# A depthwise convolution moved from VectorE to TensorE, in a two-layer hybrid decoder trunk

## What is computed

```python
p = rmsnorm(x) @ odd_w_in              # 1024 -> 1696 + 1024 columns
o_c = rwkv7(p[..., :1696])             # r, k, v (512 each), decay, a, gate (low rank)
o_d = conformer_conv(p[..., 1696:])    # a and gate, 512 channels each
x = x + concat(o_c, o_d) @ odd_w_out

def conformer_conv(h):
    a, gate = split(h)                 # 512, 512
    z = pad(a * sigmoid(gate), 30 zeros in front)
    y[n, ch] = sum_j conv_w[j, ch] * z[n + j, ch] + conv_b[ch]     # 31 taps, each channel by itself
    return silu(layernorm(y))

# rwkv7, per head of 64: S_t = S_{t-1} (diag(w_t) - kk_t^T (kk_t a_t)) + v_t^T k_t,  y_t = S_t r_t
```

## Time and profile before

| | us |
|---|---|
| time of a run, median of 3 | 1414.79 |
| span of the profiled execution | 1408.7 |
| TensorE matmul busy | 1295.4 (92%) |
| VectorE busy | 716.9 (51%) |
| ScalarE busy | 425.5 (30%) |
| GpSimd busy | 519.9 (37%) |
| second mixer, first projection matmul to first output projection tile | 584.9 to 1003.9 |

### The profile page before, as it was taken

How to read it: one execution, slowest core, us unless ns; L and a number is a source line. 1 busy time by engine, 2 the same in 40 slices (tenths; PEclk the granted TensorE clock), 3 DMA queues, 4 the chain that set the end, 5 groups by cost and what they waited for, 6 DMA issues and landing times. The chain is left out here.

```text
span 1408.7 us, 20615 instructions
## 1 busy us (share of the span) xinstructions
PE 1295.4 (92%) x8420; PEld 1034.2 (73%) x8420; DVE 716.9 (51%) x1012; ACT 425.5 (30%) x536; POOL 519.9 (37%) x374
## 2 busy tenths in 40 slices
PE   5899999999999999979798887777899999999997
PEld 4797978888888888856565666564688888888885
DVE  7435365551124534477858888585655511245333
ACT  4547333221222222254234333232432212122110
POOL 4341435554445545431121110110155544455441
PEclk9899999999999999999998999897999999999998
DMA  4321222223222223210010010000022232222321
GB/s 181 113 99 53 80 70 90 90 89 115 94 90 89 89 98 107 94 60 31 31 61 31 2 60 2 31 32 1 30 90 90 89 118 90 90 90 89 107 73 60
DMA packets 16803, 105.65 MB, mean 75 GB/s; under 512 B 1872, under 2 KB 2144, under 8 KB 4832
## 3 DMA queue, kind: packets, MB, share of 16 engines
q1 hardware_dynamic: 16304, 104.03, 21.4%
q10 hardware_dynamic: 432, 0.64, 0.1%
HBM read 102.57 MB, written 2.10 MB: 74 GB/s over the span
## 5 line engine op out<-in xcount | busy, mean ns | idle before, releaser
L484 POOL TENSOR_TENSOR w_lo<-w_raw,w_hi 128x512 fp32r<-128x512 f32 x368 | 511.1, 1420 | 846.3 <-ACT w_hi L497 296.8
L841 PE MATMUL ps<-h_hi,w_hi 128*128 128x512 f32 x696 | 285.1, 410 | 11.8 <-POOL w_lo L473 11.8
L841 PE MATMUL ps<-h_lo,w_hi 128*128 128x512 f32 x696 | 273.9, 394 | 0.0
L841 PE MATMUL ps<-h_hi,w_lo 128*128 128x512 f32 x696 | 273.5, 393 | 0.0
L841 PEld LDWEIGHTS ps<-h_hi,w_hi 128*128 128x128 f32 x696 | 132.6, 190 | 53.0 <-issue 14.1
L572 ACT ACTIVATE w_hi<-w_raw 128x2048 fp32r<-128x2048 f32 x50 | 95.6, 1912 | 201.8 <-PE ps L841 148.5
L841 PEld LDWEIGHTS ps<-h_hi,w_lo 128*128 128x128 f32 x696 | 132.3, 190 | 28.5
L841 PEld LDWEIGHTS ps<-h_lo,w_hi 128*128 128x128 f32 x696 | 132.5, 190 | 28.1 <-issue 2.7
L841 PE MATMUL ps<-f_hi,w_hi 128*128 128x512 f32 x384 | 151.7, 395 | 0.0
L841 PE MATMUL ps<-f_lo,w_hi 128*128 128x512 f32 x384 | 151.7, 395 | 0.0
L841 PE MATMUL ps<-f_hi,w_lo 128*128 128x512 f32 x384 | 151.7, 395 | 0.0
(11 more groups left out here) (300 smaller groups left out, 1991.2 us busy)
## 6 DMA issues: line engine op xcount, KB each, us to landing
w_raw<-in_weights SPq DMA_DIRECT2D x93, 1024.0 KB, 4.9
outT<-x SPq DMA_DIRECT2D x8, 256.0 KB, 2.2
x<-in_xT SPq DMA_DIRECT2D x6, 256.0 KB, 7.4
masks_f<-in_masks SPq DMA_DIRECT2D x1, 768.0 KB, 10.9
x<-in_xT ACTq DMA_DIRECT2D x2, 256.0 KB, 5.6
w_raw<-in_weights SPq DMA_DIRECT2D x1, 512.0 KB, 6.5
low_w<-in_low_w SPq DMA_DIRECT2D x1, 512.0 KB, 11.6
sgu_ln<-in_sgu_ln SPq DMA_DIRECT2D x1, 512.0 KB, 3.6
```

What stands on the lines that cost most here:

```text
L484: piece = pool.tensor_tensor(w_lo[:, j, at], w_raw[:, j, at], w_hi[:, j, at].bitcast(f32), SUB)
L841: mm = pe.matmul(bank(gb(g) if isinstance(i, int) else g % 2), w, r, start=(k == 0 and m == 0), stop=(k == K - 1 and m == 2))
```

## The change

The convolution becomes matmuls. For a channel group of 128, the stationary operand is a 128 x 128 matrix with two diagonals for each half of its rows. For pair j of 16, rows a = 0..63 carry tap 2j to output column a and tap 2j - 1 to column a + 64; rows b = 64..127 carry tap 2j to column b and tap 2j - 1 to column b - 64. The moving operand is z from position 2j on. So the even taps of a channel are summed in one half of a bank's partitions, the odd taps in the other half, one position off. The two halves of the rows are two matmuls into two banks, `gb(g)` and `gb(g + 1)`; each product is again made of three. 16 pairs make 8 steps `("conv", c, q)` of 12 matmuls of 64 rows and 512 columns. The diagonal matrices are built on the host and lie in four further 1 MB chunks among the weights (numbers 22, 24, 26, 28 of `ROWS`, each taking the place of two tiles).

z is written to `z`, copied to `z_hi` by ScalarE (in `low`), and `z_rest` on VectorE makes `z_lo`. After the last step of a group, `conv_out` on ScalarE copies the even halves to `cv` with the bias and the odd halves to `odd`, and issues two DMAs that move `odd` by 64 partitions and one position to `odd_up`; `conv_sum` on VectorE, placed five steps later, adds it to `cv`. The order of the tiles is new, and quarters or conv steps also stand after `dx` (`DX_N`). Steps per iteration: 24, 24, 24, 16; eight conv steps stand in the start. The taps' columns leave `cols`.

```diff
-MIX1 = [2] * 11
+MIX1 = [2] * 15
-ROWS = [0, 2, 4, 3, 14, 15, 5, 7, 6, 1, 16, 17, 8, 10, 9, 18, 19, 11, 13, 12, 20, 21]
+CONV = [22, 24, 26, 28]
+PAIRS = 16
+ROWS = [0, 2, 14, 15, 4, 3, 22, 23, 5, 7, 6, 16, 17, 8, 24, 25, 1, 10, 9, 11, 13, 12, 18, 19, 26, 27, 20, 21, 28, 29]
...
+        def pairs_of(c):
+            return [("conv", c, q) for q in range(8)]
+
+        ORDER1 = [("slice", t, q) for q in range(4) for t in (0, 2)] + [("stat",)] + quarters([14]) + [("spread",)] \
+            + quarters([15])[:2] + [("zw", 0)] \
+            + quarters([15])[2:] + [("za", 0), ("decay_v", 0, 0), ("ksq", 0)] + quarters([4])[:2] \
+            + [("decay", 0, 1), ("decay_v", 0, 1)] + quarters([4])[2:] + [("ks", 0), ("ks_v", 0), ("decay", 0, 2)] \
+            + [("decay_v", 0, 2)] + quarters([3]) + [("dyn", 0, 0)] + pairs_of(0)[:4] \
+            + [("dyn", 0, 1)] + pairs_of(0)[4:6] + [("bonus", 0)] + pairs_of(0)[6:]
+        FILL = {0: quarters([5, 7, 6, 16, 17, 8]), 1: pairs_of(1) + quarters([1, 10, 9, 11]),
+                2: quarters([13, 12, 18, 19]) + pairs_of(2), 3: quarters([20, 21]) + pairs_of(3)}
+
+        TX_N = {0: [1] * 6, 1: [1] * 6, 2: [1] * 5 + [0], 3: [1, 0, 1, 1, 1, 1]}
+        DX_N = {0: [1] * 6, 1: [1] * 6, 2: [1] * 5 + [0], 3: [1, 0, 1, 1, 1, 1]}
+        STATE_N = {0: [1] * 6 + [0, 0], 1: [1] * 6 + [0, 0], 2: [1] * 8, 3: [0] * 8}
...
-                ORDER1 += [("scores", c, i)] + fill(SCORE_N[c][i])
-            ORDER1 += taps[0]
+                ORDER1 += [("scores", c, i)] + fill(1)
             for lv in range(1, LEVELS):
-                ORDER1 += [("tx", c, lv, 0), ("tx", c, lv, 1)] + mid[lv] + fill(LEVEL_N[c][lv - 1])
-                ORDER1 += [("dx", c, lv, 0), ("dx", c, lv, 1)] + end[lv] + taps[lv]
+                ORDER1 += [("tx", c, lv, 0), ("tx", c, lv, 1)] + mid[lv] + fill(TX_N[c][lv - 1])
+                ORDER1 += [("dx", c, lv, 0), ("dx", c, lv, 1)] + end[lv] + fill(DX_N[c][lv - 1])
...
+            def conv_out(c):
+                g = g1(CONV[c])
+                act.wait_ge(s("gemm_done"), g + 2)
+                if c:
+                    act.wait_ge(s("odd_moved"), 32 * c)
+                act.activation(cv[0:64, c, :], bank(gb(g))[0:64], ACT.Identity, bias=col("conv_b", c)[0:64])
+                act.activation(odd[64:128, :], bank(gb(g))[64:128], ACT.Copy).then_inc(s(f"gemm_evac{g % 2}"), 1)
+                act.activation(cv[64:128, c, :], bank(gb(g + 1))[64:128], ACT.Identity, bias=col("conv_b", c)[64:128])
+                act.activation(odd[0:64, :], bank(gb(g + 1))[0:64], ACT.Copy).then_inc(s(f"gemm_evac{(g + 1) % 2}"), 1)
+                act.wait_ge(*evacuated(g))
+                act.wait_ge(*evacuated(g + 1))
+                if c:
+                    act.wait_ge(s("cv_done"), c)
+                act.dma_start(odd_up[0:64, 1:SEQ], odd[64:128, 0:SEQ - 1]).then_inc(s("odd_moved"), 16)
+                act.dma_start(odd_up[64:128, 1:SEQ], odd[0:64, 0:SEQ - 1]).then_inc(s("odd_moved"), 16)
...
+            def conv(c, q):
+                g = g1(CONV[c])
+                n = N_MIX1 + POS1[CONV[c]] // 2
+                if q == 0:
+                    pe.wait_ge(s("lo_done"), n + 1)
+                    pe.wait_ge(s("z_lo_done"), c + 1)
+                    pe.wait_ge(*freed(g))
+                    pe.wait_ge(*freed(g + 1))
+                for j in range(2 * q, 2 * q + 2):
+                    at, t = slice(P * j, P * j + P), slice(2 * j, 2 * j + SEQ)
+                    for m, (w, v) in enumerate(((w_hi, z_hi), (w_lo, z_hi), (w_hi, z_lo))):
+                        done = []
+                        for i, r in enumerate(COLUMN_HALVES):
+                            done += [pe.matmul(bank(gb(g + i)), w[r, n % 2, at], v[r, t], start=(j == 0 and m == 0),
+                                               stop=(j == PAIRS - 1 and m == 2))]
...
+            def z_rest(c):
+                dve.wait_ge(s("z_hi_done"), c + 1)
+                dve.wait_ge(s("zeroed"), 6)
+                if c:
+                    dve.wait_ge(s("gemm_done"), g1(CONV[c - 1]) + 2)
+                at = slice(TAPS - 1, TAPS - 1 + SEQ)
+                tt(z_lo[:, at], z[:, :], F(z_hi[:, at]), SUB).then_inc(s("z_lo_done"), 1)
+
+            def conv_sum(c):
+                g = g1(CONV[c])
+                dve.wait_ge(*evacuated(g))
+                dve.wait_ge(*evacuated(g + 1))
+                dve.wait_ge(s("odd_moved"), 32 * (c + 1))
+                tt(cv[:, c, 1:SEQ], cv[:, c, 1:SEQ], odd_up[:, 1:SEQ], ADD).then_inc(s("cv_done"), 1)
...
-            def taps(c, a, b):
-                for j in range(a, b):
...
-                        stt(cv[:, c, :], zpad[:, j:j + SEQ], col("conv_w", TAPS * c + j), cv[:, c, :], MUL, ADD)\
-                            .then_inc(s("tap_done"), 1)
```

More of the change, by code:

```diff
@@ L197, in build @@
             om_mu = sb("om_mu", [P, 14])
+            z_hi = sb("z_hi", [P, SEQ + TAPS + 1], f32r)
+            z_lo = sb("z_lo", [P, SEQ + TAPS + 1], f32r)
+            odd = sb("odd", [P, SEQ])
+            odd_up = sb("odd_up", [P, SEQ])
         ps = ctx.enter_context(nc.psum_tensor("ps", [P, 8, 512], f32))
@@ L316, in quarters @@
             return [("slice", t, q) for t in tiles for q in range(4)]
[L318 to L327, removed]
@@ L402, in build @@
                 held += [step[1]]
+            if step[0] == "conv" and step[2] == 7:
+                held += [CONV[step[1]]]
             scaled_yet = scaled_yet or step[0] == "spread"
@@ L410, in build @@
             for t in held:
+                if t in CONV:
+                    order += [("conv_out", CONV.index(t))]
+                    continue
                 order += [("evac_a", t), ("evac_q", t)]
@@ L425, in build @@
                 pieces += [("cut", N_MIX1 + POS1[step[1]] // 2 + 2, part) for part in range(4)]
+            if step[0] == "conv" and step[2] == 7:
+                pieces += [("cut", N_MIX1 + POS1[CONV[step[1]]] // 2 + 2, part) for part in range(4)]
         ORDER1 = order + pieces
+        order, later = [], []
+        for step in ORDER1:
+            order += [step] + [other for left, other in later if left == 1]
+            later = [(left - 1, other) for left, other in later if left > 1]
+            if step[0] == "low" and step[1] >= 15 and step[1] % 2 == 1:
+                later += [(1, ("z_rest", (step[1] - 15) // 2))]
+            if step[0] == "conv_out":
+                later += [(5, ("conv_sum", step[1]))]
+        ORDER1 = order
         def mu_col(t):
@@ L1792, in _tok, with _conv @@
     return w[:, c0:c0 + 256].reshape(KD, P, 256).transpose(1, 0, 2).reshape(P, 2048)
+def _conv(w, c):
+    t = np.zeros((P, PAIRS, P), np.float32)
+    a = np.arange(64)
+    b = a + 64
+    for j in range(PAIRS):
+        t[a, j, a], t[b, j, b] = w[2 * j, P * c + a], w[2 * j, P * c + b]
+        if j:
+            t[a, j, b], t[b, j, a] = w[2 * j - 1, P * c + a], w[2 * j - 1, P * c + b]
+    return t.reshape(P, 2048)
 def _down(w, half, d):
```

61 lines of the change are left out of this document (29 added, 32 removed).

## The result

The change makes the kernel slower: 1427.93 us (median of 4 runs, 1424.96 to 1432.01) against 1413.28 (1411.06 to 1415.5); ratio 1.0116, 95% interval 1.0094 to 1.0138, or 16 us. The forecast was 1408. The profiled execution's span is 1426.9 us.

The account below looks back on a forecast made before the run. TensorE's work, and VectorE where taps stand ahead of updates, were taken to bound the kernel by turns. Iterations -13.8, start +4.6 and dearer pairs +2.5 sum to -6.7 us: 1408 us, own range 1398 to 1418, full range 1388 to 1442.

Parts of the forecast that it names:

- Price of a step: TensorE's conv steps: a pair of half-row matmuls takes 0.243 us, a step 1.57 us plus 0.08, like a projection quarter.
- Taps off VectorE, XT waits gone: Iterations 0 to 3: VectorE loses 25 us of taps each, so late X/XT updates (8.7, 7.9, 7.0, 7.2 us) stop idling TensorE.
- What stays idle, 4.5 us an iteration: TensorE in the iterations: 4.5 us stay idle in each of iterations 0 to 2, 9.5 in iteration 3.
- The DMA, "hidden": Moving odd taps by 64 partitions: lands in 2.2 us, VectorE waits for it five steps later, about 6 us: no cost.
- Clock, 70% given back: Iterations 0 to 3: less idling returns 70% of the clock loss, 4.5, 3.7, 6.0 and 3.9 us.
- Before iteration 0, +4.6: The stage's start: 50.7 us less 9.0, plus 11.1 for eight steps and 2.5 of bank wait, gives 55.3.
- Rival 2, idle is refilled: Iterations: updates stay late, ScalarE is late for TX; half of 56 us idle stays: 1418, or 1431 without clock gain; chance 0.24.

Follow-up runs that it names:

- e6: e1 with the end of a tile's evacuation (ScalarE's part, VectorE's last product) and conv_out moved behind a level's TX copies; ratio 1.0005 to the kernel before.
- e9: e1 with the edits of e5 and e6 together; ratio 0.9964 to the kernel before.
- e11: e9 with e10's order, state-step evacuations behind the state update, rounding only behind a TensorE step and not directly ahead of TX, G or U copies; ratio 0.9916.
- e14: e11 with the bonus behind all four steps of tile 5 and conv_out(3) behind the first U copy; ratio 0.9892 to the kernel before, 1397.2 us.
- e4: The kernel before with 29 of each group's 31 taps left out and nothing added to TensorE; ratio 0.9760, 34 us less than before.
- e1: The changed kernel with ScalarE copying the odd taps straight to the other 64 partitions, without the two DMAs; ratio 1.0042 to the kernel before.
- e2: The changed kernel with the DMA kept and conv_sum of groups 0 to 2 placed 16 steps behind conv_out instead of 5; ratio 1.0070 to the kernel before.
- e3: The changed kernel with one pair of taps per conv step instead of two (half of the products left out); ratio 0.9985 to the kernel before.
- e10: e1 with tiles 1 and 5 ahead of iteration 0 in place of conv(0), which follows in iteration 0; ratio 1.0055 to the kernel before.
- e13: e11's queues with the old tile order ahead of iteration 0, four added steps there and four more in iteration 3; ratio 1.0035 to the kernel before.
- e7: e1 with the reciprocal chain (ks_v) behind tile 3's evacuation and the bonus behind the conv steps; ratio 1.0049 to the kernel before.
- after: The changed kernel itself, as profiled, without follow-up edits; 1427.93 us, ratio 1.0116 to the kernel before.
- e5: e1 with no piece of weight rounding between or directly ahead of a level's TX copies on ScalarE; ratio 1.0011 to the kernel before.
- e8: e1 with conv_out(3) placed behind the first U copy of iteration 3; ratio 1.0057 to the kernel before.

## Why the prediction was wrong

- *Price of a step*: right. Pitch 0.230, forecast 0.243; work 284.4 against 282.1 us.
- *Taps off VectorE, XT waits gone*: right (from 30.9 to 0.2 us at the levels, 3.3 to 0.5 at the state steps), VectorE at 41 to 45 us in iterations 0 to 2 as said. Two readings of the prediction are off without effect: VectorE's tenths in slices 18 to 27 are 7785888888, and in iteration 3 the taps were half of VectorE's work, not 30 to 40%.
- *What stays idle, 4.5 us an iteration*: **this step failed.** It stayed 35.0 us in place of 23.0. I reasoned from busy shares ("ScalarE is busy 31 of 92 us ... neither sets an iteration's length") and listed, apart from the four copies of conv_out(3), only waits that the old trace already had. e6, e9, e11 and e14 show what was missing: what stands ahead of the TX and G copies in ScalarE's queue once TensorE no longer pauses. e4 shows that in the old order, even without any new work, 33 us stay.
- *The DMA, "hidden"*: wrong. It cost with its issues some 10 us (e1), a part of them, by e2's median 6, as VectorE's standstill. Five steps of the order are 6 us, but counted from where ScalarE takes up conv_out; copies (2.6 us), issues (0.5 to 1.3 each) and landing (2.4) used them up. I had priced a landing of 2.2 us from the earlier trace rows and not the way to it.
- *Clock, 70% given back*: wrong, 36% (25.8 to 16.6). The loss goes with the idle time, but loosely: 8.3 us with 15.6 idle (e14), about what I had forecast for 23; 9.7 with 28.6 (e1), 14.4 with 34.3 (e3), yet 16.0 with 26.2 (e10) and 7.9 with 29.5 (e13). What else moves it stays open.
- *Before iteration 0, +4.6*: +9.4. The work of the eight steps was right (11.3 us at the upper clock, forecast 11.1). The idle time fell by 1.9 us and not by 4.7, since the bank wait was 5.8 and not 2.5: I had taken the evacuation of the earlier trace rows, without the reciprocal ahead of it. And the clock gave nothing back, where I had 1.8. How far the wait can be mended is open: e7 shortens it and the start, e10 takes it away and meets 7.1 us for rx instead. In e13 the start, with the old order of tiles and four steps more than before, took 53.9 us against 50.7 before and 61.1 in e11: the four steps took the place of the old wait for rx, for 3.2 us.
- *Rival 2, idle is refilled*, is what happened, for one of the reasons that it gave (ScalarE late for TX; the updates on VectorE were not late). It sized the idle at half of 56 us and the clock at half or nothing, 1418 to 1431. That 1427.9 lies within is partly luck: the idle time was 35 us and not 28, and 5 us came in the start, which it had left alone. 0.24 was too little for a case in which each delay was visible in the order list.

## What to carry to other kernels

Work that moves to the engine that sets the time costs nearly its full price (e3: 13.5 of 16.6 us). What the freed engine gives back is less than the waits that name it (e4: 17.1 of 30.9 us of them stayed): leave its work out and measure (34 us, where I had taken 51). Take that as an estimate for the order as it stands and not as a ceiling, since added work also fills gaps. Then walk the in-order queue of each helper engine past the change, and ask of every copy that the main engine waits for what now stands ahead of it, DMA issues and standing waits included. Compare only versions with the same queue care: here it was worth 0.7% to the old kernel too, and with it the two versions took the same time, in their profiles, in the stretches that the change touched.

## What the runs showed of the hardware

- ScalarE copied from one half of the partitions of a PSUM bank to the other half of SBUF's at an ordinary copy's price (0.59 us for 64x511), so moving a half needs no DMA.
- A DMA issue on ScalarE's queue took 0.47 to 1.30 us of that queue, and behind each of the four pairs of issues the next copy started 1.3 to 2.0 us after the one before had ended. The DMAs of 128 KB from SBUF to SBUF landed 2.4 us after their issue.
- Behind the 5.8 us wait in the start the conv pairs ran at a granted clock of 0.50, the lower level (pitch 0.43), for 3.5 us: eight of them cost what fifteen would have.
- The same steps ahead of iteration 0 took 60.1 us at a granted clock of 0.94 (after, e2, e9) and 63.8 at 0.89 (e1, e5, e6, e8), with the same idle time of 7.8. What sets which, no run here tells; a difference of 3 us between two single profiles of this stretch says nothing by itself.
- While GpSimd rounded a weight chunk (632.67 to 639.18 in after), four VectorE operations over 128x512 took 1.4 to 1.8 us each; those just before and behind took 0.7. That GpSimd is the cause is not shown.
